# A first feed-forward whose eight last up turns become seven half-size products, on one Trainium2 core

## The chip, the core and the metric

The kernel runs on one core of one Trainium2 chip, in one launch. The metric is device time in microseconds (us) of the whole kernel, median of the runs. The engines are named as in the profile: PE (TensorE, with PEld for its weight loads), DVE (VectorE), ACT (ScalarE), POOL (GpSimd) and SP (SyncE, which only issues DMAs here).

## The reference, cut to what matters

512 tokens of 1024 features pass a first block and then a second one. The first block ends in a feed-forward, the part that is changed:

```python
h = _layer_norm(x) * (1.0 + sc2) + sh2                     # 512 x 1024
u = _causal_depthwise_conv(h @ w_up[l], conv_w[l], conv_b[l])   # 512 x 5632, 3 taps
a, val = jnp.split(u, 2, axis=-1)
y = (jax.nn.silu(a) * val) @ w_down[l]                     # 2816 -> 1024
x = _layer_norm(alpha * x + (1.0 + g2) * y, ln2_g[l], ln2_b[l])
```

The second block has two more feed-forwards of the same size (528 tokens), after latent attention and after a pooling mixer.

## The kernel before, in words

All matrix products are made in float32r from two parts of each operand: hi is the operand rounded to float32r, lo is what is left. A product is three matmuls that add up in PSUM: w_lo x_hi, w_hi x_lo, w_hi x_hi (mm3, around L801 to L808). Features lie on the 128 partitions, tokens on the columns.

Weights are a stream of blocks of 128 x 1024 float32 (512 KB). A block holds 2 k-rows of 4 tiles of 128 x 128. Each passes a ring of four slots (RING) in three buffers: SP loads w_raw (load_w, L714, the DMA at L719) when GpSimd has made the lower part of the block four earlier; ScalarE copies it to w_hi (upper, L1913, the copy at L1911) when TensorE has used that slot; GpSimd subtracts into w_lo (lower, L1699). All three run behind each other in the fixed order of each engine's own program; semaphores (w_in, w_hi_ok, w_lo_ok, w_used) count blocks.

The first feed-forward's stages are up_a (4 blocks a turn, 11 turns) and down_a (12 blocks, two passes). In a turn of up_a TensorE makes four tiles of 128 features x 512 tokens (batch, two gate tiles m = 0, 2 and two value tiles m = 1, 3), block by block, so that all four end near the end of the turn, 8 k each. They lie in the four double banks PS[:, m, ...]. TensorE begins tile m of a turn when VectorE has read it (free[m]). Turn 0 is made in halves of 256 tokens by head1, turns 1 to 10 in a loop. For each turn

- ScalarE (take, in ffn, L2210): one pass per tile from PSUM with the last tap's weight and the bias (L2220), silu of the two gate tiles (L2229), rounding of the two products to mid_hi;
- VectorE (body, in ffn, L3116): the two other taps of each tile, 8 scalar_tensor_tensor of PSUM and work (L3130), two gated products (L3136), two lower parts mid_lo (L3140).

So the intermediate of 22 tiles is kept as mid_hi and mid_lo from the start, and down_a reads these. PSUM of one core holds four double banks of 1024 float32 per partition; a classic turn uses 512 of each.

TensorE's matmuls of 512 columns appear in the profile under L808, as do those of 256. The stage out ahead of up_a has its last pass in halves of 256 tokens (tail1, L1260, CUTS1).

Of the kernel before, what the change touches and what calls it, by code (L numbers as in the profile page):

```python
# [35 lines left out]
RING = 4  # L36
# [36 lines left out]
NB = {name: b for name, b, _ in STAGES}  # L73

FULL0, FREE0, _f, _u = {}, {}, 0, [0, 0, 0, 0]


# [15 lines left out]
for _name, _b, _t in STAGES:  # L93
    FULL0[_name], FREE0[_name] = _f, list(_u)
    _f += sum(n - 1 for n, _, _ in BATCH[_name]) * (1 if _name in NORMS1 else TAILS.get(_name, (_t,))[0])
    for _k in range(4):
        _u[_k] += tiles_in(_name, _k) * _t
# [61 lines left out]
def program(nc, xT, meta, stream, ada, vecs, consts, rel, rope, yT):  # L159
    with ExitStack() as ctx:  # L160
# [161 lines left out]
        def halves(name):  # L322
            return sem(name + "_a"), sem(name + "_b")
# [386 lines left out]
        def _(sp):  # L710
# [78 lines left out]
        def _(pe):  # L789
# [26 lines left out]
            def batch(name, bi, g, n, blocks, tiles, kks, cols, x, T, h_ready=None, between=None, place=None,  # L816
                      between_at=0):

                done = 0
                for bi_, b in enumerate(blocks):  # L820
# [4 lines left out]
                    for m in range(tiles):  # L825
                        if bi_ == 0:
                            begin(name, bi, m, g)
                            if place is not None:
                                place(m)
                        for k in range(kk):  # L830
                            kt = done + k
                            if m == 0 and h_ready is not None:

                                pe.wait_ge(h_ready[0], h_ready[1] + kt + 1)
                            xh, xl = x(kt)
                            last = mm3(PS[:, (BATCH[name][bi][2] + m) % 4, :], wtile(w_hi, slot, k, m, cols),
                                       wtile(w_lo, slot, k, m, cols), xh, xl, spans(T, name), bi_ == 0 and k == 0,
                                       bi_ == len(blocks) - 1 and k == kk - 1)
                        if bi_ == len(blocks) - 1 and m < tiles - 1:
                            last.then_inc(full, 1)  # L840
# [299 lines left out]

            def mid(T):
                return lambda k: (ht(mid_hi, k, T), ht(mid_lo, k, T))

# [440 lines left out]
            head1("up_a", "out", hx1, CUTS1)  # L1584
            with pe.Fori(1, 11) as g:
                batch("up_a", 0, g, g * 4 + BLK0["up_a"], range(4), 4, 2, 4, hx1, S1)

            pe.wait_ge(meta_ok, 1)
            pe.matmul(PS[:, 0, 512:512 + KD * META], ones[:, :], RS[:, 0:KD * META], start=True, stop=True)\
              .then_inc(meta_ok, 1)  # L1590
            batch("down_a", 0, 0, BLK0["down_a"], range(12), 4, DOWN_ROWS, 4, mid(S1), S1, (midl_ok, 1))
            tail1("down_a", mid(S1), DOWN_ROWS, ready_mid)
# [98 lines left out]
        def _(gp):  # L1691
# [134 lines left out]
            lower1(0)  # L1826
            lower_blocks(BLK0["up_a"] + RING, BLK0["dqkv"])
            lower_ahead("dqkv")
# [72 lines left out]
        def _(act_):  # L1901
# [245 lines left out]
            def attention2():  # L2147
# [257 lines left out]
            def behind_up():  # L2405
# [160 lines left out]
        def _(v):  # L2566
# [549 lines left out]
            def ffn(up, T, layer, y0, mid0, a=0):  # L3116

                def body(g, psum=lambda m: psumT(m, T)):
# [18 lines left out]
                    for j in range(2):  # L3137
# [3 lines left out]
                                        mid_hi[:, ds(o, T - a)].bitcast(F32), ALU.subtract).then_inc(midl_ok, 1)  # L3141
                if T == S1:
                    body(0, turn0)
                    add_means()
                    with v.Fori(1, 11) as g:
                        chain.turn(g, 4)
                        chain.base -= 4
                        body(g)
                    chain.end(11)
                else:  # L3150
                    loop(11, 4, body)

            take_first1("out", 2)
            norm1("out", 2)
            ffn("up_a", S1, 0, 0, 0)

# [478 lines left out]
```

## Time and profile before

| | |
|---|---|
| median of 3 runs | 2018.42 us (2017.65 to 2018.46) |
| span of the profiled execution, first to last instruction | 2015.8 us |
| the rest, launch and end around the span | about 2.6 us |
| TensorE busy | 1984.0 us, 98% |
| up_a turns 1 to 10, one turn | 22.71 us |
| HBM read, written | 181.03 MB, 2.10 MB |

The page gives one execution's span; the device time of an execution is a little longer than its span. TensorE's busy time is modelled from issue and pipeline, so 98% busy does not say that each matmul takes its shortest time, only that there is hardly a moment without one. What a stretch costs is read from the starts in the chain of waits.

### The profile page before, as it was taken

How to read it: one execution, taken by the hardware profiler on the slowest of the kernel's cores; microseconds unless marked ns; L12 is line 12 of the kernel's file. 1: busy time of each engine (PE TensorE's matmuls, PEld its weight loads, DVE VectorE, ACT ScalarE, POOL GpSimd, SP SyncE). 2: the span in 40 equal slices, each digit the busy share in tenths (PEclk: the TensorE clock that was granted, in tenths of full speed). 3: DMA queues.
4: the chain of work that ended last, by engine and by line, in shares of the span. 5: the costliest groups of instructions: out<-in, count | busy, mean ns of one | idle time of the engine just before them, and what ended most of it. 6: DMA issues, size and time to landing. Idle time of an engine off the chain costs nothing.

```text
span 2015.8 us, 35690 instructions
## 1 busy us (share of the span) xinstructions
PE 1984.0 (98%) x13514; PEld 1795.2 (89%) x13514; DVE 850.4 (42%) x1587; ACT 848.7 (42%) x1358; POOL 843.9 (42%) x510
## 2 busy tenths in 40 slices
PE   8999999999999999999999999999999999999997
PEld 6888888889877778999877999999999899999997
DVE  6964540227534340075677263333301663433102
ACT  3333433334644442255577453444323554443332
POOL 2536424451543445515565434343442234344442
PEclk9999999999999999999999999999999999999999
DMA  8932002221322223403100212222232112222321
GB/s 336 344 135 86 17 17 94 94 101 36 104 94 83 89 88 115 135 14 125 63 1 1 84 46 91 93 85 92 89 100 95 43 64 86 91 83 94 106 94 53
DMA packets 54958, 184.49 MB, mean 92 GB/s; under 512 B 6992, under 2 KB 10320, under 8 KB 54864
## 3 DMA queue, kind: packets, MB, share of 16 engines
q1 hardware_dynamic: 53024, 180.97, 26.3%
q10 hardware_dynamic: 1840, 2.19, 0.4%
q8 instruction: 69, 1.13, 0.2%
q14 instruction: 25, 0.20, 0.0%
HBM read 181.03 MB, written 2.10 MB: 91 GB/s over the span
## 4 chain that ended last, share of the span: by engine, by line
PE 89%; DVE 5%; ACT 2%; issue 2%; DMA 1%; SPq 1%; POOL 0%; DVEq 0%; ACTq 0%
PE PS L808 73%; PE PS L1112 2%; PE PS L926 2%; PE PS L974 2%; PE PS L1005 1%; PE PS L890 1%; PE PS L917 1%; DMA ada_w<-ada 1%; PE PS L1058 1%; PE PS L1239 1%; PE PS L1227 1%; PE PS L1649 1%; DVE work L3130 1%; ACT P L2156 1%; PE PS L902 1%
## 5 line engine op out<-in xcount | busy, mean ns | idle before, releaser
L1699 POOL TENSOR_TENSOR w_lo<-w_raw,w_hi 128x1024 fp32r<-128x1024 f32 x263 | 640.3, 2442 | 881.3 <-ACT w_hi L1911 855.5
L1911 ACT ACTIVATE w_hi<-w_raw 128x1024 fp32r<-128x1024 f32 (+2 forms) x299 | 286.8, 979 | 664.5 <-PE PS L808 618.4
L808 PE MATMUL PS<-H_hi,w_lo 128*128 128x256 f32 (+3 forms) x1952 | 515.5, 319 | 0.7 <-DVE H_lo L2707 0.3
L808 PE MATMUL PS<-H_lo,w_hi 128*128 128x256 f32 (+3 forms) x1952 | 511.4, 317 | 0.0
L808 PE MATMUL PS<-H_hi,w_hi 128*128 128x256 f32 (+3 forms) x1952 | 510.8, 316 | 0.0
L3130 DVE SCALAR_TENSOR_TENSOR work<-PS,vec,work 128x512 f32<-128x512 f32 (+4 forms) x264 | 187.2, 750 | 437.9 <-ACT work L2220 428.3
L808 PEld LDWEIGHTS PS<-H_hi,w_lo 128*128 128x128 f32 x1952 | 321.4, 188 | 35.5 <-DVE work L3130 7.9
L808 PEld LDWEIGHTS PS<-H_hi,w_hi 128*128 128x128 f32 x1952 | 321.8, 188 | 25.6
L808 PEld LDWEIGHTS PS<-H_lo,w_hi 128*128 128x128 f32 x1952 | 321.5, 188 | 24.7
L808 PE MATMUL PS<-mid_hi,w_lo 128*128 128x256 f32 (+2 forms) x968 | 228.7, 294 | 0.0
L808 PE MATMUL PS<-mid_hi,w_hi 128*128 128x256 f32 (+2 forms) x968 | 226.9, 292 | 0.0
L808 PE MATMUL PS<-mid_lo,w_hi 128*128 128x256 f32 (+2 forms) x968 | 226.6, 292 | 0.0
L808 PEld LDWEIGHTS PS<-mid_hi,w_lo 128*128 128x128 f32 x968 | 158.1, 188 | 4.6 <-issue 0.3
L808 PEld LDWEIGHTS PS<-mid_hi,w_hi 128*128 128x128 f32 x968 | 158.2, 188 | 3.9
L808 PEld LDWEIGHTS PS<-mid_lo,w_hi 128*128 128x128 f32 x968 | 158.0, 188 | 4.0
L2220 ACT ACTIVATE work<-PS,vec 128x512 f32<-128x512 f32 (+1 forms) x132 | 103.5, 784 | 78.2 <-PE PS L808 78.2
L3198 DVE TENSOR_SCALAR work<-PS 128x256 f32<-128x256 f32 (+1 forms) x12 | 5.2, 431 | 126.9 <-ACT work L2025 126.9
L3190 DVE TENSOR_TENSOR RS<-work 128x528 f32<-128x528 f32 (+1 forms) x3 | 2.1, 704 | 134.1 <-ACT work L1992 134.1
L2229 ACT ACTIVATE work<-work 128x512 f32<-128x512 f32 (+1 forms) x66 | 41.4, 631 | 41.0 <-DVE work L3130 41.0
L2867 DVE TENSOR_REDUCE small<-PS 72x1 f32<-72x528 f32 (+3 forms) x80 | 42.0, 525 | 29.5 <-PE PS L976 29.1
L1005 PE MATMUL PS<-PT,V 128*128 128x272 f32 (+1 forms) x192 | 54.0, 379 | 0.4 <-DVE work L2893 0.3
L2654 DVE SCALAR_TENSOR_TENSOR XC<-ada_w,cond,XC 128x1024 f32<-128x1024 f32 x24 | 53.0, 2207 | 1.3
(422 smaller groups left out, 3036.9 us busy)
## 6 DMA issues: line engine op xcount, KB each, us to landing
w_raw<-stream SPq DMA_DIRECT2D x289, 512.0 KB, 3.2
ada_w<-ada SPq DMA_DIRECT2D x48, 512.0 KB, 6.9
X<-xT SPq DMA_DIRECT2D x8, 256.0 KB, 6.4
yT<-X SPq DMA_DIRECT2D x16, 128.0 KB, 1.7
rel_raw<-rel ACTq DMA_DIRECT2D x4, 256.0 KB, 2.7
vec<-vecs ACTq DMA_DIRECT2D x1, 390.0 KB, 3.6
sin_t<-rope ACTq DMA_DIRECT2D x1, 264.0 KB, 2.8
cos_t<-rope ACTq DMA_DIRECT2D x1, 132.0 KB, 2.5
```

Of the source, the lines that this page charges most:

```text
L808: last = pe.matmul(out[:, c0 + a:c0 + b], w, x[:, a:b], start=start and i == 0, stop=stop and i == 2)
L926: last = pe.matmul(o_psum1(par), pt_part1(n, par)[:, j * QB:(j + 1) * QB], v_head1(p, par, j), start=j == 0, stop=j == i, skip_group_check ...
L974: pe.matmul(out[0:qn, c0 + a:c0 + b], l[:, o + q0:o + q0 + qn], r[:, o + a:o + b], start=j == 0, stop=False, skip_group_check=True)
L1005: return pe.matmul(o_psum2(par, late)[:, a - a0:b - a0], v_weights2(p, par, j), pt2(par, j, a, b), start=j == 0, stop=stop, skip_group_che ...
L1112: last = pe.matmul(PS[:, t, 0:512], l[:, hs], r[:, wr], start=kt == 0 and j == 0, stop=kt == 7 and j == 2)
L1699: gp.tensor_tensor(w_lo[:, o], w_raw[:, o], w_hi[:, o].bitcast(F32), ALU.subtract)\
L1911: return act_.activation(out, in_, ACT.Copy, scale=scale)
L2220: act_.activation(ht(work, m, T)[:, a:], u(m)[:, a:], ACT.Identity, bias=v1("conv", g * 16 + (c + 3)), scale=v1("conv", g * 16 + (c + 2)))\
L2229: act_.activation(y, y, ACT.Silu).then_inc(s_ok, 1)
L2654: ins = v.scalar_tensor_tensor(to, w, cond[:, k:k + 1], a, ALU.mult, ALU.add)
L2867: v.tensor_reduce(small[0:qn, t % 2:t % 2 + 1], scores2(t), AX.X, ALU.max, negate=True)\
L3130: ins = v.scalar_tensor_tensor(y[:, b:], u[:, b - s:T - s], w, y[:, b:], ALU.mult, ALU.add)
```

## The change

Turns 0 to 2 of up_a stay as they are (CLASSIC = 3). For turns 3 to 10 (FAST = 8) the product of a 1024 x 512 weight part with the 1024 x 512 activations is made by a Winograd form of Strassen's scheme: both are cut in 2 x 2 parts, and seven products of half size in each direction, with sums of parts on both sides, take the place of eight. The parts along the contraction are the even and odd k, along the tokens the halves of 256 (QUAD), along the features the first and last 256 of the block's columns.

- TensorE (product): 7 products p = 0 to 6 of 4 k x 2 halves c x 3 matmuls of 256 columns. They add up in parts of one double bank per c; even and odd turns use different pairs of banks. Products 2, 4 and 6 add onto product 0's sums, product 5 onto product 3's; between them ScalarE copies sums out (keep) and VectorE adds them in (join).
- Weights: of one turn's four blocks SP loads five quarters-of-matrix pieces of 512 KB in lines of 1 KB (load_fast), and GpSimd issues two DMAs that add a piece onto one in SBUF (add_sums). VectorE makes two further sums in w_s2 (sum2, sum4). ScalarE rounds all seven (fast_upper), GpSimd makes the lower parts of 0, 1, 4, 5, 6, VectorE those of 2 and 3 (fast_lower).
- Activations: the four sums D5, D7, D6, D4 with their hi and lo parts are made once, between VectorE's turns 1 and 2 (operands, lower_operands). Conv weights of the value tiles change sign where the scheme gives the negative.
- The intermediate is kept in float32 (mid_f); its rounding (round_mid) and lower parts (lower_mid) are made when down_a starts, three of 22 in the last fast turn and the rest behind it, since their room is that of the pieces above. down_a's tiles 2 and 3 wait for the last turn's taps (begin_down_a).

```diff
+def load_fast(f):                                     # SP
+    n = WIN0 + 4 * f
+    for x, (i, j) in ((0, (0, 0)), (None, (1, 0)), (2, (0, 0)), (1, (0, 1)), (3, (1, 1))):
+        if x is None:
+            if f:
+                sp.wait_ge(fast_lo, W_0 + 2 * (f - 1) + 2)
+            else:
+                wait_own_room_read(sp)
+            sp.dma_start(quad_out(w_s1[:, :]), quadrants(n, i, j)).then_inc(s1_in, 16)
+            continue
+        sp.wait_ge(w_lo_ok, n + {0: 0, 1: 1, 2: 2, 3: 3}[x] + 1)
+        if f and x < 2:
+            sp.wait_ge(s2_ok, 2 * (f - 1) + x + 1)
+        sp.dma_start(quad_out(raw_part(x)), quadrants(n, i, j)).then_inc(w_in[(n + x) % RING], 16)
...
-            with pe.Fori(1, 11) as g:
+            for g in range(1, CLASSIC):
                 batch("up_a", 0, g, g * 4 + BLK0["up_a"], range(4), 4, 2, 4, hx1, S1)
...
+def product(f, p):                                    # TensorE
+    q = 7 * f + p
+    wait_lo(pe, f, p)
+    if f == 0 and p in (2, 3, 4, 6):
+        pe.wait_ge(dl_ok, D_0 + {2: 1, 3: 2, 4: 3, 6: 4}[p])
+    part = (2, 0, 2, 1, 2, 1, 2)[p]
+    for c in range(2):
...
+        for i in range(4):
+            o = fast_slot(q) * BLK + i * QUAD + c * P
+            wh, wl = w_hi[:, o:o + P], w_lo[:, o:o + P]
+            xh, xl = moving(p, i)
+            for j, (w, x) in enumerate(((wl, xh), (wh, xl), (wh, xh))):
+                last = pe.matmul(acc_of(f, c, part), w, x, start=p in (0, 1, 3) and i == 0 and j == 0,
+                                 stop=i == 3 and j == 2, skip_group_check=True)
...
+for f in range(FAST):
+    consumed(CLASSIC + f - 1)
+    for p in range(7):
+        if f == 0 and p == 1:
+            consumed(CLASSIC, (0, 1))
+        elif f == 1 and p == 0:
+            consumed(CLASSIC, (2, 3))
+        product(f, p)
...
+add_sums(0, 1)                                        # GpSimd
+add_sums(0, 3)
+fast_lower(0, 0)
+fast_lower(0, 1)
+for f in range(FAST):
+    fast_lower(f, 4)
+    if f + 1 < FAST:
+        add_sums(f + 1, 1)
+    fast_lower(f, 5)
+    fast_lower(f, 6)
+    if f + 1 < FAST:
+        add_sums(f + 1, 3)
+        fast_lower(f + 1, 0)
+        fast_lower(f + 1, 1)
...
+gp.wait_ge(s1_in, 16 * (f + 1))                       # add_sums(f, 1)
+gp.dma_start(quad_out(w_s1[:, :]), quadrants(WIN0 + 4 * f, 1, 1), accum_op=ALU.add).then_inc(s1_sum, 16)
...
+for f in range(FAST):                                 # ScalarE, ffn1
+    g = CLASSIC + f
+    fast_upper(f, 3)
+    if f:
+        fast_tap(f - 1, 2)
+        fast_tap(f - 1, 3)
+        gate_silu(g - 1, 0)
+    keep(f, 1, 0)
+    keep(f, 1, 1)
+    fast_upper(f, 4)
+    if f:
+        gate_silu(g - 1, 1)
+    fast_upper(f, 5)
+    keep(f, 2, 0)
+    keep(f, 2, 1)
+    fast_upper(f, 6)
+    keep(f, 5, 0)
+    keep(f, 5, 1)
+    if f + 1 < FAST:
+        fast_upper(f + 1, 0)
+        fast_upper(f + 1, 1)
...
+    fast_tap(f, 0)
+    fast_tap(f, 1)
+    if f + 1 < FAST:
+        fast_upper(f + 1, 2)
...
+body(0, turn0)                                        # VectorE, ffn1
+add_means()
+body(1, psum1)
+operands()
+lower_operands()
+sum2(0)
+body(2, psum1)
+for f in range(FAST):
+    g, u = CLASSIC + f, (lambda m: fast_u(f, m))
+    fast_lower(f, 2)
+    fast_lower(f, 3)
+    if f:
+        taps(g - 1, 1, lambda m: fast_u(f - 1, m))
+    sum4(f)
+    if f:
+        gated(g - 1, 0)
+        gated(g - 1, 1)
+    join(f, 4, 0)
+    join(f, 4, 1)
+    if f + 1 < FAST:
+        sum2(f + 1)
+    else:
+        for k in range(3):
+            lower_mid(k)
+    join(f, 5, 0)
+    join(f, 5, 1)
+    taps(g, 0, u)
+taps(10, 1, lambda m: fast_u(FAST - 1, m))
+gated(10, 0)
+gated(10, 1)
+for k in range(3, KF):
+    lower_mid(k)
```

## Rows read from the trace of the kernel before

**Rows 1.** The page, busy time, share and instructions of each engine.

```profile
PE 1984.0 (98%) x13514; PEld 1795.2 (89%) x13514; DVE 850.4 (42%) x1587; ACT 848.7 (42%) x1358; POOL 843.9 (42%) x510
```

**Rows 2.** The chain of waits, turn 3 of up_a: start us, us, what.

```profile
580.99 19.90 PE PS L808 x84
...
601.06 0.79 ACT work L2220
...
601.99 0.76 DVE work L3130
...
603.70 19.90 PE PS L808 x84
```

**Rows 3.** Windows, one up turn and the stretch before turn 1, with columns.

```profile
core 0: us, PE busy (x) PEld busy (x) DVE busy (x) ACT busy (x) POOL busy (x), PEclk, DMA share, GB/s
...
580.99:603.70 22.71, 22.66 (x97) 17.88 (x97) 8.12 (x13) 9.53 (x12) 9.56 (x4) 1.00 0.26 91
...
495.43:508.40 12.97, 11.98 (x92) 11.12 (x91) 11.14 (x33) 9.92 (x22) 0.00 (x0) 1.00 0.00 1
```

**Rows 4.** The chain of waits in the tail of out, halves of 256.

```profile
463.83 2.82 PE PS L808 x24
...
473.55 2.83 PE PS L808 x24
```

**Rows 5.** Groups by form, 480 to 860 us: busy us, mean ns, idle before.

```profile
L1911 ACT ACTIVATE w_hi<-w_raw 128x1024 fp32r<-128x1024 f32 x64 | 66.3, 1053 | 151.0 <-PE PS L808 151.0
...
L1911 ACT ACTIVATE mid_hi<-work 128x512 f32 x20 | 12.3, 633 | 7.2 <-DVE work L3136 7.2
...
L1911 ACT ACTIVATE gate<-PS 128x256 f32<-128x256 f32 x1 | 0.4, 385 | 0.9 <-PE PS L1248 0.9
...
L2229 ACT ACT_TABLE_LOAD x1 | 1.3, 1283 | 0.0
...
L3130 DVE SCALAR_TENSOR_TENSOR work<-PS,vec,work 128x511 f32<-128x511 f32 x44 | 31.9, 745 | 133.6 <-ACT work L2220 133.5
...
L3140 DVE TENSOR_TENSOR mid_lo<-work,mid_hi 128x512 f32 x20 | 12.9, 688 | 3.2 <-ACT mid_hi L1911 3.2
...
L3074 DVE TENSOR_TENSOR H_lo<-work,H_hi 128x256 fp32r<-128x256 f32 x11 | 4.6, 422 | 1.5 <-ACT H_hi L1911 1.5
```

**Rows 6.** Lines with minimum, median and maximum ns; a page group; a piece of timeline.

```profile
L3136 DVE TENSOR_TENSOR work<-work x22: 678/682/1054, 517.0 to 743.9; 128x512 f32<-128x512 f32 x22
...
L3113 DVE TENSOR_TENSOR X<-X,gate x8: 677/680/2328, 521.0 to 526.8; 128x512 f32<-128x512 f32 x8
...
L1699 POOL TENSOR_TENSOR w_lo<-w_raw,w_hi x64: 2386/2400/3384, 508.9 to 842.2; 128x1024 fp32r<-128x1024 f32 x64
...
L2654 DVE SCALAR_TENSOR_TENSOR XC<-ada_w,cond,XC x24: 1283/1287/3392, 54.0 to 113.9; 128x1024 f32<-128x1024 f32 x24
...
L2654 DVE SCALAR_TENSOR_TENSOR XC<-ada_w,cond,XC 128x1024 f32<-128x1024 f32 x24 | 53.0, 2207 | 1.3
...
746.42 2.37 DVE L3162 TENSOR_SCALAR RS<-RS 128x16 f32<-128x16 f32 x1
...
746.37 2.40 POOL L1699 TENSOR_TENSOR w_lo<-w_raw,w_hi 128x1024 fp32r<-128x1024 f32 x1 [8.48 <-ACT w_hi L1911]
```

**Rows 7.** DMA: issues, the queue over the span and at the end; SP in the chain.

```profile
w_raw<-stream SPq DMA_DIRECT2D x289, 512.0 KB, 3.2
...
q1 hardware_dynamic: 53024, 180.97, 26.3%
...
q1 hardware_dynamic: 2016, 1.84, 33.7%
...
11.33 1.05 SPq L728
```

**Rows 8.** The timeline at turn 1 and turn 2, VectorE and ScalarE.

```profile
538.96 1.28 DVE L3136 TENSOR_TENSOR work<-work 128x512 f32<-128x512 f32 x2
...
554.25 0.78 ACT L2220 ACTIVATE work<-PS,vec 128x512 f32<-128x512 f32 x1 [0.49 <-PE PS L808]
```

More of the change, by code:

```diff
@@ L94 @@
     FULL0[_name], FREE0[_name] = _f, list(_u)
-    _f += sum(n - 1 for n, _, _ in BATCH[_name]) * (1 if _name in NORMS1 else TAILS.get(_name, (_t,))[0])
+    _f += sum(n - 1 for n, _, _ in BATCH[_name]) * (1 if _name in NORMS1 else TAILS.get(_name, (TOLD.get(_name, _t),))[0])
     for _k in range(4):
@@ new lines, in acc_of, with fast_u, e_buf, quadrants @@
+        def acc_of(f, c, part):
+            o = QUAD * part
+            return PS[:, 2 * (f % 2) + c, o:o + QUAD]
+        def fast_u(f, m):
+            return PS[:, 2 * (f % 2) + m % 2, 512 * (m // 2):512 * (m // 2) + 512]
+        def e_buf(kind, c):
+            if kind == 5:
+                return e5[:, c * QUAD:(c + 1) * QUAD]
+            o = QUAD * (2 * c + kind - 1)
+            return w_e[:, o:o + QUAD]
+        def quadrants(n, i, j):
+            return stream[n:n + 4, :, j * 512 + i * QUAD:j * 512 + (i + 1) * QUAD].rearrange("a p c -> p a c")
@@ L1584, in _, with consumed, moving @@
             head1("up_a", "out", hx1, CUTS1)
-            with pe.Fori(1, 11) as g:
+            for g in range(1, CLASSIC):
                 batch("up_a", 0, g, g * 4 + BLK0["up_a"], range(4), 4, 2, 4, hx1, S1)
+            def consumed(g, tiles=range(4)):
+                for m in tiles:
+                    pe.wait_ge(free[m], free_before("up_a", 0, m, g) + 1)
+            def moving(p, i):
+                if p in (2, 3, 4, 6):
+                    hi, lo = {2: (D6_hi, D6_lo), 3: (D5_hi, D5_lo), 4: (D7_hi, D7_lo), 6: (D4_hi, D4_lo)}[p]
+                    return hi[:, i * QUAD:(i + 1) * QUAD], lo[:, i * QUAD:(i + 1) * QUAD]
+                k, t = {0: (2 * i, 0), 1: (2 * i + 1, 0), 5: (2 * i + 1, 1)}[p]
+                return tuple(x[:, t * QUAD:(t + 1) * QUAD] for x in hx1(k))
@@ L1590, in _, with begin_down_a @@
               .then_inc(meta_ok, 1)
-            batch("down_a", 0, 0, BLK0["down_a"], range(12), 4, DOWN_ROWS, 4, mid(S1), S1, (midl_ok, 1))
+            def begin_down_a(m):
+                if m >= 2:
+                    pe.wait_ge(free[m - 2], FREE0["down_a"][m - 2] + 1)
+            batch("down_a", 0, 0, BLK0["down_a"], range(12), 4, DOWN_ROWS, 4, mid(S1), S1, (midl_ok, 1),
+                  begin_tile=begin_down_a)
             tail1("down_a", mid(S1), DOWN_ROWS, ready_mid)
@@ L1826, in _, with add_sums, fast_lower @@
             lower1(0)
-            lower_blocks(BLK0["up_a"] + RING, BLK0["dqkv"])
+            lower_blocks(BLK0["up_a"] + RING, WIN0)
+            def add_sums(f, part):
+                if part == 1:
+                    gp.wait_ge(s1_in, 16 * (f + 1))
+                    gp.dma_start(quad_out(w_s1[:, :]), quadrants(WIN0 + 4 * f, 1, 1), accum_op=ALU.add).then_inc(s1_sum, 16)
+                else:
+                    wait_raw(gp, f, 2)
+                    gp.dma_start(quad_out(raw_part(2)), quadrants(WIN0 + 4 * f, 1, 0), accum_op=ALU.add).then_inc(s3_sum, 16)
+            def fast_lower(f, p):
+                wait_hi(gp, f, p)
+                q = 7 * f + p
+                gp.tensor_tensor(fast_part(w_lo, q), fast_src(p), fast_part(w_hi, q).bitcast(F32), ALU.subtract)\
+                  .then_inc(lo5_ok if p == 5 else w_lo_ok, 1)
+            add_sums(0, 1)
[12 more added lines that the diff above has]
+                    fast_lower(f + 1, 1)
+            lower_blocks(BLK0["down_a"], BLK0["dqkv"])
             lower_ahead("dqkv")
@@ new lines, in gate_silu, with round_mid @@
+            def gate_silu(g, j):
+                wait_out(act_, "up_a", 0, 2 * j, g)
+                y = ht(work, 2 * j, S1)
+                act_.activation(y, y, ACT.Silu).then_inc(s_ok, 1)
+            def round_mid(k):
+                act_.wait_ge(mid_ok, k + 1)
+                if k < 3:
+                    act_.wait_ge(lo5_ok, LO5_0 + FAST)
+                elif k < 5:
+                    act_.wait_ge(c_ok, E_0 + 4 * FAST)
+                else:
+                    act_.wait_ge(w_used, BLK0["down_a"] + RING)
+                copy(ht(mid1_hi, k, S1), ht(mid_f, k, S1)).then_inc(midh_ok, 1)
@@ L3141, in body @@
                                         mid_hi[:, ds(o, T - a)].bitcast(F32), ALU.subtract).then_inc(midl_ok, 1)
[L3142 to L3151, printed above, removed]
+                loop(11, 4, body)
```

262 lines of the change are left out of this document (255 added, 7 removed).

## The prediction, made before the changed kernel ran

> **What bounds the kernel now.** First the busy shares [rows 1]: TensorE is busy 98% of 2015.8 us, the others 42% each. The chain of waits [rows 2] has the same shape in every up turn: 84 matmuls, one ScalarE tap, one or two VectorE taps, and TensorE again 22.71 us after the last time. The windows [rows 3] show that TensorE has no hole there: 22.66 of 22.71 us busy, VectorE 8.12, ScalarE 9.53, GpSimd 9.56, the granted clock 1.00 (2.4 GHz). A turn is 4 tiles x 8 k x 3 = 96 matmuls of 512 columns, 0.2366 us each. In this stage the end moves only with TensorE's columns, as long as 11 to 14 us of slack on the other engines lasts. The profiled span is 2015.8 us, the median of the runs 2018.4; I make the sum on the span's intervals and add it to the median. About 0.2% (4 us) can be told from no change.
>
> **What it removes on TensorE.** A fast turn has 7 products x 4 k x 2 column halves x 3 = 168 matmuls of 256 columns, in place of 96 of 512. Runs of 24 such matmuls, exactly one product, took 2.82 and 2.83 us in the tail of out, where the halves are 256 wide [rows 4], each matmul with its own weight load. I take 2.83: 7 x 2.83 = 19.81 us against 22.71, so 2.90 a turn and **-23.2 us** for eight turns. That is all the change can give; 2.82 would make it 23.8.
>
> **What it adds beside it, per fast turn.**
> - ScalarE: 9.53 minus two mid_hi (1.24) and four roundings of 1024 columns (4 x 1.05), plus seven roundings (7.35) and six keeps from PSUM at the 0.385 us of a 256-column copy (2.3): 13.8 of 19.8 us [rows 3, 5].
> - VectorE: 8.12 minus two mid_lo (1.38), plus two lower parts and two sums of 1024 columns. No row has that form. From 0.42 for 256 and 0.68 for 512 columns [rows 5, 6], 1.22 each, 4.9 together. Four joins: 0.42 twice, 0.75 twice (the taps' row), 2.3. Sum 13.9 us.
> - GpSimd: five lower parts at 2.40 are 12.0 us instead of 9.6, and two accumulating DMAs, issued from its queue.
> - DMA: seven pieces of 512 KB instead of four, in lines of 1 KB: 3.67 MB in 19.8 us, 185 GB/s. Lines up to 2 KB moved 1.84 MB at a share of 33.7% in 16 us, so about 340 GB/s when full; the 4 KB lines give the same (180.97 MB at 26.3% of the span) [rows 7]. Half of the DMA stands idle: bandwidth costs nothing.
> - TensorE's new waits: product 2 waits for ScalarE's keeps of product 0, with product 1 and half of another between (4.2 us) for two copies of 0.385 behind a rounding, two taps and a silu (3.3): nothing, and 0.9 us short of something. Product 6 waits for the joins behind product 4, with product 5 (2.8) as cover for 0.42: nothing.
> - SP: five loads a turn instead of four, each behind a wait; the wait of w_s1 holds up the pieces 2, 1 and 3 queued behind it, which are wanted 11 us later or more: nothing.
>
> By busy time each engine fits. By order it is tight, since VectorE and GpSimd block each other. A VectorE sum over two SBUF inputs takes 0.68, but 2.33 when it starts inside a GpSimd lowering; one of 1024 columns takes 1.28 alone and 3.39 at worst, 2.21 in the mean beside GpSimd; even a 16-column one lasted 2.37 us next to a 2.40 us lowering, and GpSimd's own reach 3.38 [rows 6]. The Trainium skill, SBUF — State Buffer, on engine ports, says the shared pair is an exclusive lock, held for the whole instruction, which also covers a VectorE op with two SBUF inputs against a GpSimd op that reads SBUF. The trace agrees. So 12.0 us of GpSimd and 4.9 + 1.4 (the two gated products) = 6.3 us of VectorE queue for one resource: 18.3 of 19.8 us. The taps and joins, with one input in PSUM, are free of it.
>
> The loop that decides: last lower part of a turn (fast_lower f+1, 1) on GpSimd; then two VectorE lower parts (2.4); only then may SP reload w_s1 (3.2 to landing [rows 7], 3.7 with the queue's hop, for four times as many lines); GpSimd's add_sums waits for that and blocks what is behind it: issue a, lower part 5, 6, issue a, lower parts 0 and 1 of the next turn. Round: 2.4 + 3.7 + 4 x 2.4 + 2a = **15.7 + 2a**, hidden if a is under 2.05 us. **a** is not in the trace: GpSimd issues no DMA. Lower bound: SP's issues of 128 lines, 1.05 us [rows 7]. Upper: four times that for 512 lines, 4.2. I take 1.7, nearer to the one real row: 19.1, hidden under TensorE, but with 0.7 us to spare, so I charge 0.3 a turn, **+2.4**. The accumulate's landing, 3.2 to 6.4 us (it also reads what it writes), gates sum2 and the joins behind it on VectorE; walking the order through a turn, TensorE feels it past about 5.5.
> The Trainium skill, DMA: Bandwidth & Descriptors, latency table, gives GpSimd's path a first byte at about 1 us; with a = 1 the loop would be 17.7 us and the 0.3 would go. No run here shows it.
>
> **Entry.** Before turn 2's taps VectorE makes the operands: four sums, D5, D7 (1.22 each), D6, D4 (1.28), four lower parts (the last four behind ScalarE's roundings), sum2: 14.8 us of two-input work from 540.2 (end of its turn 1 work [rows 8]), with at least one GpSimd lowering in between (2.4): to 558.5 or 560.9. Then ScalarE rounds product 2's weights (1.05) and takes turn 2's first tap at 560.4 to 562.8; before it was 554.3. VectorE's taps of tiles 0 and 1 end at 563.6 to 566.0; product 1 was due at 561.1. Taps, gated products and lower part 2 (VectorE, behind all of it) end at 569 to 573; product 2 was due at 564.0. So 5 to 9 us of hole, without the lock 3.4. I take **+7**. What a hole of 3 us does to the clock no row shows; between 495 and 508 us TensorE idled 1 us of 13 and the clock stayed 1.00 [rows 3], so I add nothing.
>
> **Exit.** The 22 roundings and 22 lower parts of the intermediate leave the turns (0.63 and 0.69 each); three pairs go into turn 10, 19 run behind it. down_a eats two k per 5.7 us, the two engines make one per 0.7, so only the first is late: k = 3, wanted 6.4 us after the last product, comes behind taps, two silus, a weight rounding and the table load (1.28) at 7.0, or 9.4 with a lowering before it. 0.6 to 3 us, **+1.5**. Before, no window or wait shows a loss here.
>
> **Sum**: -23.2 + 2.4 + 7 + 1.5 = -12.3: 2018.4 - 12.3 = 2006.
>
> **Rivals.**
> 1. *GpSimd becomes the bound* (slower side). The turn is 15.7 + 2a from a = 2.05. With entry and exit (8.5) the change breaks even where a turn costs 22.71 - 1.06 = 21.65, **a = 3.0**. At a = 3.5: 22.7 a turn, nothing gained, 2027; at 4.2: 24.1, +11 + 8.5, 2038. For it: 512 lines per DMA; against: only a scaling in full proportion to the lines gets there.
> 2. *Half the gain*: a of 2.4 to 2.9, or a landing of 6 to 7 us: 20.5 to 21.5 a turn, 2009 to 2017. Nothing in the trace excludes it.
> 3. *No lock trouble at all*: GpSimd's and VectorE's pieces interleave by luck, entry 3.4, exit 0.6, no charge: -19.2, 1999.
> 4. *It doesn't do what it says*: 256-column matmuls wait for weight loads outside the tails of rows 4. TensorE would take more than 2.83 per product. In the stages of rows 4 the pace holds over 24 in a row; I give it 2%.
>
> **Chances.** Forecast (2001 to 2009) 0.42, rival 3 0.07, rival 2 0.23 (a quarter of it within 0.2% of before), rival 1 0.26, rival 4 0.02. Faster 0.64, same 0.09, slower 0.27. The range 1999 to 2027 leaves out the far part of rival 1 and a little below; the forecast's own range is 2001 to 2009.
>
> **What would show it.** PE busy near 1961 us at about 14090 matmuls (13514 + 8 x 72); fast turns of 19.8 to 20.1 us in the chain, TensorE released by VectorE only in turn 3 and once in down_a. GpSimd's lowerings lengthened where VectorE's sums stand, mean above 2.5 us. If fast turns are over 21 us and TensorE waits for GpSimd's w_lo, a or the lock is the cause; if it waits for lower part 2, the landing. A hole under 3 us at turn 3 would make the entry wrong.

## The result and the profile after

The changed kernel took 2030.15 us in the median of 4 runs (2025.31 to 2031.86), beside 2018.44 us for the kernel before (4 runs, 2017.65 to 2019.02): a ratio of 1.0054 [1.0041, 1.0066], **11.7 us slower** (0.5%). That lies above the forecast of 2006 and above the top of its range, 2027. The profiled execution of the changed kernel is the slowest of its four (2031.86), so its span stands 14.3 us above that of before, and not 11.7.

The page of the changed kernel, its busy line and the DMA issues, answers to [rows 1] and [rows 7]:

```profile
span 2030.1 us, 36641 instructions
...
PE 1973.2 (97%) x14090; PEld 1819.5 (90%) x14090; DVE 962.1 (47%) x1664; ACT 883.7 (44%) x1434; POOL 887.0 (44%) x534
...
L2052 POOL TENSOR_TENSOR w_lo<-w_raw,w_hi 128x1024 fp32r<-128x1024 f32 x32 | 84.6, 2708 | 71.3 <-ACT w_hi L2153 71.3
...
w_s<-stream SPq DMA_DIRECT2D x8, 512.0 KB, 3.4
w_s<-stream POOLq DMA_DIRECT2D x8, 512.0 KB, 8.8
w_raw<-stream POOLq DMA_DIRECT2D x8, 512.0 KB, 8.1
```

TensorE made the 14090 matmuls forecast, but was busy for 1973 us instead of 1961. GpSimd's two DMAs a turn took 8.8 and 8.1 us to land in the median, where SP's plain piece of the same size took 3.4.

Where the time went is read from marks in the chain of waits, since TensorE's runs stand in it with their starts. On the way into the stage nothing was lost: TensorE's unbroken run into turn 1 began at 507.76, before at 508.38. Turn 3 of the kernel before begins at 558.27 (the stretch of [rows 2] that begins at 580.99 is turn 4, not 3), so the first fast turn was due at 557.65 and its product 2, back to back, at 563.3. Product 0 began at 557.90, product 1 at 563.60 and product 2 at 568.64: the **entry** cost 5.3 us. From there the 54 products left ended at about 746.1, after 177.5 us; at 2.83 each they would have taken 152.8: the **steady turns** cost 24.7 us. From the last product to a mark inside down_a (the first stretch at the line of the swapped products, 852.97 before and 864.75 now) it took 118.6 us, against 112.9 from the end of turn 10 before: the **exit** cost 5.7. So -23.2 + 5.3 + 24.7 + 5.7, less 0.6 for the earlier start, is about +11.9, and the marks show +11.8. The other 2.5 us of this execution stand behind the mark, in stages that the change leaves alone: 1.1 of them at the start of the next stage, where one of ScalarE's DMA issues took 1.34 us instead of 0.45 and a weight part came late; the rest is scattered.

The chain of waits over one fast turn has nothing of TensorE in it, where [rows 2] had 19.90 of 22.71 us on it:

```profile
590.85 2.28 DVE w_lo L3566 x2
...
593.15 3.34 DMA w_s<-stream
...
596.77 11.48 DMA w_s<-stream
...
608.27 0.03 DVE w_s L3575
...
609.41 0.70 DVE PS L3592
...
610.14 0.79 ACT work L2471
...
610.95 1.43 DVE work L3520 x2
...
612.41 1.41 DVE work L3520 x2
613.81 2.28 DVE w_lo L3566 x2
```

Read from the top: VectorE's lower parts 2 and 3 of one turn; then SP may reload w_s1 (3.34); then GpSimd's DMA adds the second piece onto it, 11.48 us from issue to landing; then sum2 (L3575), the join behind it, a ScalarE tap, VectorE's taps, and the lower parts of the next turn. The round is 22.96 us (590.85 to 613.81), of which 11.5 are everything but that landing. TensorE only follows.

In this round sum2 itself takes 1.23 us. It does not in all of them:

```profile
L3575 DVE TENSOR_TENSOR w_s<-w_s,w_raw x8: 1225/3973/4766, 555.4 to 720.2; 128x1024 f32<-128x1024 f32 x8
```

Where the landing is shorter, 8.4 to 9.0 us, sum2 takes 4.5 to 4.8 (four turns of the seven behind the first); where it is longer, 9.6 to 11.5, sum2 takes 1.2 to 1.7 (three turns). Landing and sum together are 11.3 to 13.6 us in all seven.

TensorE's windows, with the columns of [rows 3]: all turns from the entry to turn 10, one stretch behind a hole, one round, and the last part of the landing of 11.48.

```profile
557.90:731.49 173.59, 155.39 (x1227) 152.85 (x1227) 119.04 (x134) 93.51 (x143) 106.28 (x50) 0.95 0.65 152
593.15:596.50 3.35, 3.35 (x19) 3.35 (x18) 3.31 (x5) 1.35 (x2) 2.39 (x1) 0.50 0.48 157
593.15:616.11 22.96, 21.90 (x171) 21.53 (x170) 13.86 (x19) 12.54 (x20) 14.60 (x7) 0.93 0.68 161
604.00:608.30 4.30, 4.30 (x39) 4.30 (x38) 0.03 (x1) 0.20 (x1) 3.01 (x2) 1.00 1.03 229
```

TensorE stood idle for 18.2 of 173.6 us, and what it was busy with took longer than it should: 1227 matmuls at the pace of the unbroken turns measured below (20.11 us for 168) are 146.9 us, not 155.4. The granted clock shows why: 0.95 in the mean, and 0.50 (1.2 GHz) from 593.15 to 596.50, just behind a hole of 2.50 us. So TensorE's lost time is 18.2 us of holes and, by this estimate, 8.5 us of slower matmuls. That is what its time went into, not two causes: in a round whose chain has no TensorE in it a quicker TensorE would only have waited longer, and no run here shows what the end would gain at full clock.

The last window matters too. The DMA engines' share is 0.65 in the mean, but 1.03 while sum2 waits for the landing, and they moved 229 GB/s then. The forecast had half of the DMA idle and 340 GB/s when full.

### The profile page after: what moved, and what is told of

It reads as the page before. It is cut to its first block, busy times and chain, and to the rows that moved or that the text cites. A ratio compares the mean times of both kernels' runs of the same rounds, so it can differ in the third digit from the quotient of the medians.

```text
span 2030.1 us, 36641 instructions
## 1 busy us (share of the span) xinstructions
PE 1973.2 (97%) x14090; PEld 1819.5 (90%) x14090; DVE 962.1 (47%) x1664; ACT 883.7 (44%) x1434; POOL 887.0 (44%) x534
## 4 chain that ended last, share of the span: by engine, by line
PE 81%; DVE 9%; DMA 5%; issue 3%; ACT 2%; POOL 0%; ACTq 0%; DVEq 0%
PE PS L956 63%; DMA w_s<-stream 4%; PE PS L1263 2%; PE PS L1077 2%; DVE work L3520 2%; PE PS L1125 1%; PE PS L1156 1%; PE PS L1209 1%; PE PS L1041 1%; DVE w_lo L3566 1%; PE PS L1068 1%; PE PS L1380 1%; PE PS L1392 1%; PE PS L1859 1%; PE PS L1018 1%
## 5 line engine op out<-in xcount | busy, mean ns | idle before, releaser
L956 PE MATMUL PS<-H_hi,w_lo 128*128 128x256 f32 (+3 forms) x1696 | 413.5, 307 | 1.2 <-POOL w_lo L1909 0.9
L956 PE MATMUL PS<-H_hi,w_hi 128*128 128x256 f32 (+3 forms) x1696 | 410.0, 305 | 0.0
L956 PE MATMUL PS<-H_lo,w_hi 128*128 128x256 f32 (+3 forms) x1696 | 410.0, 305 | 0.0
L3495 DVE SCALAR_TENSOR_TENSOR work<-PS,vec,work 128x512 f32<-128x512 f32 (+2 forms) x176 | 125.4, 754 | 301.3 <-ACT work L2585 294.8
L2585 ACT ACTIVATE work<-PS,vec 128x528 f32<-128x528 f32 (+1 forms) x88 | 69.2, 786 | 53.9 <-PE PS L956 53.9
L1775 PE MATMUL PS<-D_hi,w_lo 128*128 128x256 f32 x256 | 76.4, 298 | 15.3 <-ACT w_e L2153 13.3
L1775 PE MATMUL PS<-D_lo,w_hi 128*128 128x256 f32 x256 | 75.2, 294 | 0.0
L1775 PE MATMUL PS<-D_hi,w_hi 128*128 128x256 f32 x256 | 75.0, 293 | 0.0
L3520 DVE SCALAR_TENSOR_TENSOR work<-PS,vec,work 128x511 f32<-128x511 f32 (+1 forms) x88 | 61.9, 745 | 11.8 <-ACT work L2471 8.8
L1775 PEld LDWEIGHTS PS<-D_hi,w_lo 128*128 128x128 f32 x256 | 51.7, 202 | 17.5 <-DVE w_lo L3566 15.7
```

Source lines behind the costliest of these rows:

```text
L956: last = pe.matmul(out[:, c0 + a:c0 + b], w, x[:, a:b], start=start and i == 0, stop=stop and i == 2)
L1775: last = pe.matmul(acc_of(f, c, part), w, x, start=p in (0, 1, 3) and i == 0 and j == 0, stop=i == 3 and j == 2, skip_group_check=True)
L2585: act_.activation(ht(work, m, T)[:, a:], u(m)[:, a:], ACT.Identity, bias=v1("conv", g * 16 + (c + 3)), scale=v1("conv", g * 16 + (c + 2)))\
L3495: ins = v.scalar_tensor_tensor(y[:, b:], u[:, b - s:T - s], w, y[:, b:], ALU.mult, ALU.add)
L3520: ins = v.scalar_tensor_tensor(y[:, s:], u(m)[:, 0:S1 - s], w, y[:, s:], ALU.mult, ALU.add)
```

## The experiments

Two theories stood at the start. **Landing** (theory L in the expectations of e1 to e4, rival A later): the adding DMAs land too late for sum2 and what stands behind it. **Lock** (rival K, then theory S): sum2 and sum4 come when GpSimd is at work, and wait for the two engines' shared access to SBUF. The forecast's rival 1 (GpSimd's issues make it the bound) was answered by the trace alone: an adding issue of 512 lines took 1.30 us in the median and 1.84 at most, not the 3.0 at which that rival decides.

In every experiment L numbers differ by some lines from the changed kernel's; sum2 is the VectorE operation `w_s<-w_s,w_raw` or `w_s<-w_s1b,w_raw` named first, sum4 the one named after it. Both take 1.22 us where nothing is in their way; "caught" stands for a sum that takes far longer beside GpSimd.

**e1: the first GpSimd DMA as a plain copy.** One half of the sum is left out by it.

```diff
-gp.dma_start(quad_out(w_s1[:, :]), quadrants(...), accum_op=ALU.add).then_inc(s1_sum, 16)
+gp.dma_start(quad_out(w_s1[:, :]), quadrants(...)).then_inc(s1_sum, 16)
```

> The piece that GpSimd's DMA adds onto w_s1 is written over it instead (plain, same queue, same 512 lines of 1 KB, same semaphores); the sum is left out. Theory L (the adding DMA's landing of 9.0 us is in the turn's loop: reload of w_s1 3.4, landing 9 to 11, sum2 1.2, join 0.7, tap 0.8, four taps 2.8, two lower parts 2.3, sum 23): the landing falls to 4 or 5 us, the loop to 18 or 19, TensorE's 19.8 to 20.5 bounds the turn, total 2005 to 2011. Rival Q (the slowness is that of GpSimd's queue, whatever it carries): landing stays at 8 to 9 us, total 2028 to 2032. Rival B (DMA traffic as a whole, seven pieces a turn): landing 7 to 8, total about 2025.

Measured: 2033.77 us (2029.27 to 2036.67, 4 runs), 1.0072 [1.0055, 1.0090] of the kernel before. **e2: that DMA left out altogether**, with every wait for it made one for SP's piece; the half sum is left out.

> GpSimd's adding DMA onto w_s1 is left out, and with it that half of the sum; who waited for it waits for SP's load. One adding DMA per turn (raw part 2) stays. Theory L: loop of 23 loses 9 us, TensorE bounds the turn, 2004 to 2009. Rival K (GpSimd's and VectorE's shared SBUF access holds up sum2 and the lower parts, and the landing is only in parallel to that): the turn stays above 21.5, total over 2018.

Measured: 2034.45 us (2030.82 to 2038.17, 4 runs), 1.0089 [1.0072, 1.0105]. The landing of that DMA is gone, and nothing came back. The operations on w_s in e1, with duration minimum, median and maximum in ns:

```profile
L2043 POOL DMA_DIRECT2D w_s<-stream x8: 807/812/947, 541.3 to 716.4; - x8
L3575 DVE TENSOR_TENSOR w_s<-w_s,w_raw x8: 3415/6821/6981, 555.3 to 722.4; 128x1024 f32<-128x1024 f32 x8
```

and in e2 the timeline of one round, first VectorE, then GpSimd:

```profile
597.82 0.43 DVE L3587 TENSOR_TENSOR PS<-PS,e 128x256 f32<-128x256 f32 x1 [0.99 <-PE PS L1775]
598.17 6.60 DVE L3574 TENSOR_TENSOR w_s<-w_s,w_raw 128x1024 f32<-128x1024 f32 x1
604.69 1.28 DVE L3591 TENSOR_TENSOR PS<-PS,w_e 128x512 f32<-128x512 f32 x2
...
597.62 1.31 POOL L2045 DMA_DIRECT2D w_raw<-stream  x1
598.44 5.23 POOL L2051 TENSOR_TENSOR w_lo<-w_raw,w_hi 128x1024 fp32r<-128x1024 f32 x2
```

The sum, 1.22 us of work, waits for nothing in data. It starts while GpSimd issues its second DMA, and ends only when *both* lowerings behind that issue are done. One lowering would have cost it 2.4. While it hangs, the joins, the taps and the next turn's sums hang behind it on VectorE.

The landing has left the loop in e2, and yet its rounds take 23.6 to 23.9 us, because the caught sum closes another loop, now through TensorE:

```profile
611.02 10.37 PE PS L1775 x72
...
621.76 1.11 DVE w_s L3574
622.87 5.71 issue
628.58 0.70 DVE PS L3591
...
630.64 1.73 ACT w_hi L2152 x2
```

TensorE, the sum (its 5.71 us of block stand as "issue"), a join, ScalarE's tap, two weight roundings and two more taps, and TensorE again at 634.91. In e1 too the sum stands straight behind a join, and not behind the landing, in five of the seven turns from 579 us on.

How sharp the condition is shows in e2's first full turn: at 578.28 its sum began 0.08 us after the start of that issue (578.20), with the same two lowerings behind it, took 1.22, and the next sum followed 19.9 us later. In e1 and e2 the sums that began 0.16 us or more after the start of the issue took 6.1 to 7.0.

**e3: both adding DMAs left out**, and both half sums with them.

```diff
-wait_raw(gp, f, 2)
-gp.dma_start(quad_out(raw_part(2)), quadrants(WIN0 + 4 * f, 1, 0), accum_op=ALU.add).then_inc(s3_sum, 16)
```

> Both adding DMAs of every turn are left out, with the half sums that they make; five plain pieces per turn remain. What is left over the best case is not DMA. Theory L: turns at 19.8 to 20.2 us, holes of entry and exit as before (about 10 us together), total 2002 to 2006, at most 3 us below the kernel with only the first left out. Rival B: clearly below it, by 5 us or more. Rival K: above 2015.

Measured: 2007.14 us (2005.88 to 2009.61, 4 runs), 0.9948 [0.9931, 0.9964]. The chain of waits shows TensorE without a break over 52 products, 2.85 us each:

```profile
568.89 148.16 PE PS L1775 x1248
```

So TensorE's step was priced right, and entry and exit together leave a gain; all that makes the change slow hangs on the two DMAs. In this kernel sum2 still met two lowerings one behind the other, but without an issue ahead of them, and took 2.88 us in the median (1.28 to 3.42): it got in between two lowerings.

**e4: a second room for w_s1, and the first adding DMA moved ahead of lower part 4**, against the landing alone; nothing is left out.

```diff
+def s1_room(f):
+    return w_s1b if f in (1, 3, 5) else w_s1
...
-                fast_lower(f, 4)
                 if f + 1 < FAST:
                     add_sums(f + 1, 1)
+                fast_lower(f, 4)
```

> Nothing is left out. A second room for w_s1 (odd turns 1, 3, 5 of the fast ones), so that SP reloads it a turn earlier, and GpSimd issues the adding DMA ahead of lower part 4 instead of behind it, some 5 us earlier. Theory L: the landing leaves the loop, turns fall from 23.1 to 20 to 21, total 2008 to 2014. Rival B: the DMA rings are full in the middle of a turn (share 0.9 to 1.0), so the landing only stretches or piece 1 comes later, total 2022 or more.

Measured: 2036.73 us (2035.87 to 2041.28, 4 runs), 1.0101 [1.0084, 1.0118]. The landing fell to 6.0 us, but SP's load of the piece still stands in its queue behind the last turn's piece 3 and this turn's piece 0, so GpSimd now waits, with the lowerings behind it; the waits of the stage, summed, with their number and the longest:

```profile
ACT work L2480 <- DVE PS L3601: 31.4, 6, 8.0
POOL w_s L2052 <- DMA w_s<-stream: 31.3, 4, 11.3
```

The second room was used too late to test anything. The test of the lock is **e5: e2, and GpSimd held** ahead of its second issue and of lower parts 0 and 1 until sum2 is done. (The half sum stays left out as in e2.)

```diff
 if f + 1 < FAST:
+    gp.wait_ge(s2_ok, 2 * (f + 1) + 1)
     add_sums(f + 1, 3)
     fast_lower(f + 1, 0)
     fast_lower(f + 1, 1)
```

> The kernel with GpSimd's first adding DMA left out (2034 us) and one wait more: GpSimd issues its other adding DMA and makes lower parts 0 and 1 of the next turn only when VectorE's sum2 is done. Work left out: half of the sum w_s1. Theory S (sum2 starts beside GpSimd's DMA issue and gets no SBUF access until the two lower parts queued behind the issue are done, 6.9 us instead of 1.2, and joins, taps and the next turn follow it): sum2 at 1.2 to 3.4, turns near 20, total 2006 to 2012. Rival A (the adding DMA's landing of 8.3 us or its traffic is what costs a turn its 3 us): a wait more can't help, total 2033 to 2042, since lower part 0 comes later.

Measured: 2010.36 us (2009.01 to 2012.30, 5 runs), 0.9961 [0.9946, 0.9976]: a wait *added* to GpSimd took 24 us off e2. The chain and the sums:

```profile
585.02 20.11 PE PS L1775 x168
```

```profile
L3575 DVE TENSOR_TENSOR w_s<-w_s,w_raw x8: 1215/1216/3415, 556.2 to 700.9; 128x1024 f32<-128x1024 f32 x8
L3581 DVE TENSOR_TENSOR w_s<-w_s,w_raw x8: 1215/1216/3414, 570.4 to 713.3; 128x1024 f32<-128x1024 f32 x8
```

**e10: the hold alone** in the changed kernel, nothing left out (the edit of e5 without that of e2).

> The changed kernel with one wait more and nothing else: GpSimd issues its second adding DMA and makes lower parts 0 and 1 of the next turn when sum2 is done. Nothing is left out. The reload of w_s1 still waits for this turn's lower part 3, so sum2 still comes some 4 us late by the landing. Theory S with the landing as second term: sum2 1.2 to 2.4 us instead of 4, but lower part 0 then waits for the late landing: turns 21.5 to 23, total 2018 to 2030. If the landing is no term at all: 2010 as with the half sum left out. If the landing is all: 2030 or more.

Measured: 2032.12 us (2029.80 to 2034.65, 4 runs), 1.0070 [1.0055, 1.0085]. The sum is short again (median 1.23 us), yet nothing is gained, and the time lies above the 2018 to 2030 of the expectation; the chain has the landing and then GpSimd's held lower part:

```profile
596.24 9.60 DMA w_s<-stream
...
605.86 1.24 DVE w_s L3576
...
607.38 1.29 POOL w_raw L2046
608.67 2.42 POOL w_lo L2052
...
611.23 4.62 PE PS L1775 x24
```

**e6: e4's order with the hold**, the second adding DMA between lower parts 5 and 6, nothing left out.

> Nothing is left out. Second room for w_s1, first adding DMA ahead of lower part 4, second one between lower parts 5 and 6, lower parts 0 and 1 of the next turn held until sum2 is done. Theory S with the landing as second term: sum2 never queues behind two lower parts, landings of 8 to 9 us end before they are wanted; turns 20 to 21, total 2008 to 2016. Rival A: over 2025, because rings are as full as before.

Measured: 2021.14 us (2017.96 to 2023.51, 10 runs), 1.0010 [1.0000, 1.0020]. The timeline of one round, VectorE, then GpSimd:

```profile
642.31 3.24 DVE L3586 TENSOR_TENSOR w_s<-w_s,w_raw 128x1024 f32<-128x1024 f32 x1
...
640.72 1.30 POOL L2055 DMA_DIRECT2D w_raw<-stream  x1
641.54 2.92 POOL L2061 TENSOR_TENSOR w_lo<-w_raw,w_hi 128x1024 fp32r<-128x1024 f32 x1
```

With one lowering behind the issue instead of two the sum takes 3.2 us in place of 6.6. The kernel is still 5 us above the 2008 to 2016 expected: a round of its chain (from 600.53) has the caught sum (3.35), the held lower part 0 (2.41) and TensorE (14.45), one behind the other, 20.8 us and more.

**e7: both DMAs kept, but 8 columns wide** (4 KB for 512; most of both half sums is left out), which separates what the issue does from what the bytes do.

> GpSimd's two adding DMAs per turn stay in their places, but carry 8 columns (128 lines of 32 bytes) instead of 512 KB; what they don't add is left out. Theory S: the issue still stands ahead of lower parts 0 and 1 and the landing is short, so sum2 meets it: sum2 above 4 us, total over 2020. Rival A: issue is cheap, traffic gone, 2005 to 2009 as with no adding DMAs at all (2007.1).

Measured: 2015.53 us (2012.47 to 2020.77, 10 runs), 0.9988 [0.9978, 0.9998]. The issue still took 0.87 us for 128 lines in place of 512, and the landing 4.3 and 3.7 us for 4 KB. The sum was short in some turns (2.02 us, arriving ahead of the issue) and in others was caught as before:

```profile
622.04 6.09 DVE L3575 TENSOR_TENSOR w_s<-w_s,w_raw 128x1024 f32<-128x1024 f32 x1
...
621.41 0.86 POOL L2046 DMA_DIRECT2D w_raw<-stream  x1
622.02 5.02 POOL L2052 TENSOR_TENSOR w_lo<-w_raw,w_hi 128x1024 fp32r<-128x1024 f32 x2
```

The bytes are not needed for the block. What decides is where the sum falls. Both expectations missed, over 2020 and 2005 to 2009: with the sum caught in every other turn the time lies between them.

**e8: both remedies, nothing left out.** Two rooms for w_s1 by the turn's parity; SP loads the next turn's piece ahead of piece 3 of this one; GpSimd adds onto it a whole turn early, behind lower part 1; and the hold. GpSimd's loop, without the rooms, the loads and the first turn:

```diff
 for f in range(FAST):
     fast_lower(f, 4)
-    if f + 1 < FAST:
-        add_sums(f + 1, 1)
     fast_lower(f, 5)
     fast_lower(f, 6)
     if f + 1 < FAST:
+        gp.wait_ge(s2_ok, 2 * (f + 1) + 1)
         add_sums(f + 1, 3)
         fast_lower(f + 1, 0)
         fast_lower(f + 1, 1)
+        if f + 2 < FAST:
+            add_sums(f + 2, 1)
```

> Nothing is left out. Two rooms for w_s1, reloaded a whole turn ahead (SP issues it ahead of piece 3), its adding DMA behind lower part 1 where GpSimd is idle, GpSimd's other adding DMA and lower parts 0 and 1 held until sum2 is done. Both terms are out: sum2 under 2.5 us, turns of 20.1 to 20.6, total 2010 to 2014, faster than before by 0.2 to 0.4%. If DMA traffic is a third term (seven pieces, two of them at 102 ns per line): turns over 21, total over 2018.

Measured: 2011.00 us (2010.25 to 2011.93, 5 runs), 0.9961 [0.9947, 0.9975]. The chain is TensorE's, turn after turn (627.46 20.12, 647.64 20.12, each with 168 matmuls), and the adding DMAs land in 5.8 to 6.3 us. SP issues its loads further from them: around the adding DMA of 623.59 at 621.55 and 627.34, where around that of 596.77 in the changed kernel two stood within 0.8 us (596.37 and 597.50).

**e11: e8 without the hold ahead of the issue and of lower parts 0 and 1** (it stands behind them, ahead of the early add alone).

> The 2011.0 us kernel without its hold: w_s1 is loaded and summed a turn ahead, but GpSimd issues its other adding DMA and makes lower parts 0 and 1 as soon as it can, and waits for sum2 only behind them. Nothing is left out. Theory S: sum2 finds its operands in time and meets the issue and the two lower parts, 6 to 7 us instead of 1.2; turns of 23 to 24, total 2028 to 2036, although no landing is late. Rival (the landing is what mattered, the hold little): 2011 to 2015.

Measured: 2027.18 us in the median, from 2013.24 to 2038.13 in 8 runs, 1.0046 [1.0016, 1.0075]; just below the 2028 to 2036 expected. No other kernel here scattered so. Its profile is of one of the quick ones, 2014.49 us, and even there the sum was caught in two of the five turns from 618 us on (the other three took 2.03, 1.25 and 2.04). In both the sum began 0.63 us after the start of the issue; at 598.42 it began with the issue, and took 1.22. A few tenths of a microsecond decide:

```profile
618.31 6.50 DVE L3592 TENSOR_TENSOR w_s<-w_s1b,w_raw 128x1024 f32<-128x1024 f32 x1
...
680.41 6.50 DVE L3592 TENSOR_TENSOR w_s<-w_s,w_raw 128x1024 f32<-128x1024 f32 x1
```

**e12: e8 with the issue let go and only the lowerings held.** It asks whether the issue itself keeps VectorE out.

```diff
-gp.wait_ge(s2_ok, 2 * (f + 1) + 1)
 add_sums(f + 1, 3)
+gp.wait_ge(s2_ok, 2 * (f + 1) + 1)
 fast_lower(f + 1, 0)
```

> The 2011.0 us kernel with its hold moved one place: GpSimd issues the adding DMA at once, and only lower parts 0 and 1 wait for sum2. Nothing is left out. If the block comes from lower parts that stand ready behind an issue, sum2 stays under 3.4 us and the total is 2009 to 2013. If the issue itself keeps VectorE from SBUF, sum2 is 1.3 us longer at most; if it blocks until GpSimd's next instruction is done, this kernel hangs back at over 2020.

Measured: 2008.78 us (2006.54 to 2009.87, 4 runs), 0.9944 [0.9927, 0.9960]. One round, VectorE, then GpSimd:

```profile
617.95 1.22 DVE L3592 TENSOR_TENSOR w_s<-w_s1b,w_raw 128x1024 f32<-128x1024 f32 x1
...
617.35 1.28 POOL L2060 DMA_DIRECT2D w_raw<-stream  x1
619.26 4.76 POOL L2066 TENSOR_TENSOR w_lo<-w_raw,w_hi 128x1024 fp32r<-128x1024 f32 x2 [0.63 <-DVE w_s L3592]
```

The sum begins 0.60 us into the issue, as in e2 and e7, and takes its 1.22 us. So the issue alone does not block it; an issue with lowerings ready behind it does. The issue need not run any more when the sum arrives: in the changed kernel the four sums of 4.5 to 4.8 us began 1.1 to 1.3 us behind its end, inside the first of the two lowerings, and waited for both. TensorE's chain in e12 is unbroken over 1248 matmuls, 148.16 us, as in e3; e8's is broken once a turn, where TensorE waits for what the hold delays.

**The exit.** In the changed kernel the timeline at the end of the last turn, VectorE, then GpSimd:

```profile
740.77 7.11 DVE L3596 TENSOR_TENSOR mid_lo<-mid_f,mid_hi 128x512 fp32r<-128x512 f32 x3
...
741.71 5.63 POOL L1909 TENSOR_TENSOR w_lo<-w_raw,w_hi 128x1024 fp32r<-128x1024 f32 x2
```

The three early lower parts of the intermediate, 0.69 us each [rows 5], took 7.1 together (1.5, 2.9 and 2.9), beside GpSimd's last lowering of the turn and its first two for down_a. No issue stands ahead of these, and each lower part waits for one lowering, as e3's sum does. The last join, the taps and the gate follow them. **e9: e8, with GpSimd held there too.**

```diff
+gp.wait_ge(midl_ok, 1 + 3)
 lower_blocks(BLK0["down_a"], BLK0["dqkv"])
```

> The kernel before this in the list, and GpSimd begins down_a's first lower parts only when VectorE has made the first three lower parts of the intermediate, which it blocked for 5 us in the changed kernel. Exit hole from 5 to 6 us down to 2 to 3: 2 to 3 us below the one without it, 2007 to 2012. Rival: down_a's first weights are then late and nothing is gained.

Measured: **2008.02 us** (2006.83 to 2008.39, 5 runs), 0.9945 [0.9932, 0.9959], the quickest kernel of the study that leaves nothing out, 3.0 us below e8. In the chains the way from the join behind the last product to the long run of down_a is 13.5 us in e9 (720.65 to 734.11) and 16.2 in e8 (722.98 to 739.20), so 2.8 us of it are the exit's. (e8's profile also starts the whole stage 2.8 us late, at 510.62 against 507.86, where the two kernels are the same, so their spans are no clean measure of it.) The page of e9 and the end of its chain, to be held against the 758.00 us at which the changed kernel began the same run of 675 matmuls:

```profile
PE 1966.6 (98%) x14090; PEld 1814.5 (90%) x14090; DVE 950.0 (47%) x1664; ACT 885.6 (44%) x1434; POOL 885.4 (44%) x534
```

```profile
720.99 1.12 DVE mid_lo L3614 x2
...
734.11 106.80 PE PS L970 x675
```

The four kernels that leave nothing out, as a table:

| us | sum2 free to be caught | GpSimd held |
|---|---|---|
| added in the turn, room reused | 2030.2 | 2032.1 (e10) |
| two rooms, added a turn ahead | 2027.2, 2013 to 2038 (e11) | 2011.0 (e8) |

Either remedy alone gives nothing that holds, both give 19 us.

## Why the prediction was wrong

**The step that failed** is the steady charge, "so I charge 0.3 a turn, +2.4". It came to 24.7 us, about 3 a turn and ten times as much. Behind it stood the claim that the deciding loop runs through GpSimd, "15.7 + 2a". With the measured a of 1.30 that loop is 18.3 us and hidden under 20.1: GpSimd was not the bound. The loop that bounds is another, and its members were all in the forecast, but priced apart: VectorE's lower parts, SP's reload, the landing, sum2, join, taps. Everything but the landing is 11.5 us. Two of its terms were wrong.

- *Landing.* Bounded at 3.2 to 6.4 us; it took 9.0 in the median of the stage and up to 11.5, and 5.8 to 6.3 where e5 and e8 issue it apart from SP's loads. Behind it stands "bandwidth costs nothing": the mean share was 0.65, but 0.88 over the landing of 11.48, and 1.03 at its end. That the crowd of loads is what stretches it is read from these shares and starts; no run has only the loads moved. "TensorE feels it past about 5.5" was wrong as well: with a free sum, 11.5 + landing passes 20.1 only at 8.6.
- *Lock.* It was seen, with its shortest and longest rows (0.68 and 2.33, 1.28 and 3.39 [rows 6]), and charged as a share of time: 18.3 of 19.8 us fit. But what it costs depends on where a sum falls. No row of before has a GpSimd issue with operations behind it, and there a 1.22 us sum takes up to 7.0. With a landing of 6.3 the loop of 11.5 + 6.3 would have been 17.8, but e1 shows what came: the sum now met the issue, took 6.8, and closed the loop through TensorE instead, 23.0 to 24.8 us from sum to sum. A late landing carries the sum past the lowerings, a shorter one leads it into them. The two terms cover each other, which is why neither came out by itself. The Trainium skill, SBUF — State Buffer, section SBUF: two separate sides, has the lock held for the whole instruction. The trace agrees for a single lowering (1.22 becomes at most 3.4), but e2's 6.6 us across two of them is more than that rule gives.

**What held.** TensorE's price: 2.85 us a product over 52 of them in e3 and e12, 2.87 in e5 and e8, for 2.83 forecast; so the gain at stake was 20.8 to 22 us, not 23.2. Rival 4 falls: the pace holds over 1248 in a row. The sum of 1024 columns: 1.22 forecast, 1.215 measured. The issue a: 1.30, inside 1.05 to 4.2 and under the 1.7 taken. The entry: 5.3 us, inside 5 to 9 and under the 7 taken. The sign of busy time: each engine fits, as forecast; e8, e9 and e12 show that the same work, in another order, runs under TensorE.

**What was off in size.** The exit, 5.7 us against 1.5 (0.6 to 3): I had the first three lower parts at 0.69 each, and they stood beside three lowerings. The same lock again, and e9's exit was 2.8 us shorter than e8's. And the clock: I added nothing for it, but behind a hole of 2.50 us it fell to 0.50; TensorE's busy time grew by an estimated 8.5 us, of which no run shows how much reached the end.

**The rivals.** The measured 2030 lies between rival 1's 2027 and 2038, but not by its mechanism, an a above 3 us. The mechanism stood in rival 2, "a landing of 6 to 7 us", whose time I put at 2009 to 2017; the landing and the lock together passed what I had let either do. The chance of slower, 0.27, stood almost wholly on the wrong cause, so that this time lies in rival 1's reach is luck. The marks that I had named for a wrong forecast did speak: turns over 21 us, with TensorE waiting for VectorE's lower part 2 (17.7 us in sum), "the landing"; that reading was half of the truth, as e1 and e2 show.

What stays open: why two lowerings behind an issue both go first, and why without an issue ahead of them they let VectorE in between (2.88 us in e3, 2.9 at the exit); what the lower clock cost the end; e12's shorter hold together with e9's at the exit, and an order in which VectorE makes sum2 ahead of the joins, weren't tried.

## What to carry to other kernels

Where VectorE operations with two SBUF inputs share a turn with GpSimd, don't add busy times: place each one against GpSimd's queue, and ask what it meets if it comes half a microsecond later. A mean share of the DMA engines says as little: look at it over the one transfer that is waited for. A loop must be walked through every engine and DMA in it with the landing as its own term, and a remedy for one of its terms can look worthless until the other is mended too, so try them crossed. A wait added to an engine off the path can be the cheapest repair.

## What the runs showed of the hardware

- A VectorE sum of two SBUF tiles of 1024 columns takes 1.215 us; beginning 0.16 to 1.1 us after the start of a GpSimd DMA issue with two ready lowerings behind it, 6.1 to 7.0 us (e1, e2, e4, e7, e11); 2.5 to 2.9 us after it, 4.5 to 4.8 (the changed kernel); within 0.1 us of it, 1.22 to 1.25 (once in e2, twice in e11). With one lowering behind the issue 3.2 (e6), with none ready 1.22 (e12).
- An adding DMA of 512 KB in lines of 1 KB, issued by GpSimd, lands in 5.8 to 6.3 us in the medians of e5 and e8, and in 8.1 to 9.0 in those of the changed kernel (11.5 at most), where SP issues loads within a microsecond of it; a plain one on that queue in 6.3 among the same loads (e1), and 4 KB still need 3.7 to 4.3 (e7). Its issue takes 1.30 us, 0.81 when it doesn't add, 0.87 for 128 short lines.
- The granted clock was 0.50 for 3.35 us behind a hole of 2.50 us in the turns, and 1.00 again in the window from 604 us on; the mean over the stage was 0.95.
- Without the hold the runs of one program on the same data spread over 25 us (e11), with it over 2 (e8). The mean granted clock of e11's runs went with their time, from 0.997 in the quickest to 0.990 in the slowest.
